# A transformer kernel: the memory cross-attention in three float32r products, with GpSimd making two of the low parts

## What is computed

```python
def memory_cross_attention(h, mem_n, w_mem_q, w_mem_kv, w_mem_o):
    q = jnp.einsum("bsd,de->bse", h, w_mem_q).reshape(B, S, MEM_HEADS, MEM_HEAD_DIM)
    kv = jnp.einsum("bmd,de->bme", mem_n, w_mem_kv)
    k = kv[..., :D_MODEL].reshape(B, M, MEM_HEADS, MEM_HEAD_DIM)
    v = kv[..., D_MODEL:].reshape(B, M, MEM_HEADS, MEM_HEAD_DIM)
    s = jnp.einsum("bshd,bmhd->bhsm", q, k).astype(jnp.float32) * (MEM_HEAD_DIM ** -0.5)
    p = jax.nn.softmax(s, axis=-1).astype(v.dtype)
    o = jnp.einsum("bhsm,bmhd->bshd", p, v).reshape(B, S, D_MODEL)
    return jnp.einsum("bse,ed->bsd", o, w_mem_o)
```

## Time and profile before

| | |
|---|---|
| median of 3 runs | 1484.01 us (1483.98 to 1484.23) |
| the profiled execution | 1484.37 us, its span 1482.6 us |
| PE busy | 1440.1 us, 97% of the span |
| DVE, ACT, POOL busy | 851.4, 552.9 and 990.2 us |
| first score matmul to first matmul of `mem_o` | 1045.72 to 1077.01 us |

### The profile page before, as it was taken

One profiled execution on the slowest core, in us unless ns is written; L12 is line 12 of the kernel. 1 busy time (PEld: TensorE's weight loads), 2 busy tenths in 40 slices (PEclk: granted clock), 3 DMA queues, 4 the chain that ended last, 5 costly groups with the idle time before them and its releaser, 6 DMA issues.

```text
span 1482.6 us, 18612 instructions
## 1 busy us (share of the span) xinstructions
PE 1440.1 (97%) x6987; PEld 1169.7 (79%) x6987; DVE 851.4 (57%) x1334; ACT 552.9 (37%) x1075; POOL 990.2 (67%) x400
## 2 busy tenths in 40 slices
PE   3999999999999999999999999999999999999997
PEld 3888877778898888888898844789789888888886
DVE  6998156554565555666744786441516555465655
ACT  3201133433454344444333376452424523333214
POOL 1857554355668899888568996365153989788653
PEclk9999999999999999999999999999999999999999
DMA  9875321223543332322443200133024323232131
GB/s 349 298 270 209 100 85 57 86 86 106 169 153 114 114 113 87 114 86 85 156 126 109 86 1 1 59 125 123 7 86 142 114 86 114 86 114 86 57 97 74
DMA packets 103385, 167.88 MB, mean 113 GB/s; under 512 B 3917, under 2 KB 61185, under 8 KB 102785
## 3 DMA queue, kind: packets, MB, share of 16 engines
q1 hardware_dynamic: 100176, 160.45, 31.7%
q10 hardware_dynamic: 3121, 6.26, 1.4%
HBM read 161.97 MB, written 4.72 MB: 112 GB/s over the span
## 4 chain that ended last, share of the span: by engine, by line
PE 84%; DVE 10%; ACT 3%; DMA 2%; issue 1%; POOL 1%; DVEq 0%; SPq 0%; ACTq 0%; POOLq 0%
PE bank L911 25%; PE bank L913 25%; PE bank L912 25%; DVE bank L2054 2%; DMA ada_w<-in_w_ada 1%; DVE smx L2507 1%; DVE x L2050 1%; PE bank L1372 1%; PE bank L1429 1%; PE bank L1448 1%; DVE bank L2050 1%; PE bank L1183 1%; DVE m L2050 1%; ACT junk L1541 1%; PE bank L1195 1%
## 5 line engine op out<-in xcount | busy, mean ns | idle before, releaser
L911 PE MATMUL bank<-ht_hi,w_hi 128*128 128x512 f32 (+1 forms) x1200 | 442.9, 369 | 0.5 <-DVE ht_lo L2050 0.3
L912 PE MATMUL bank<-ht_hi,w_lo 128*128 128x512 f32 (+1 forms) x1200 | 440.1, 367 | 0.0
L913 PE MATMUL bank<-ht_lo,w_hi 128*128 128x512 f32 (+1 forms) x1200 | 440.0, 367 | 0.0
L759 POOL TENSOR_TENSOR w_lo<-w_raw,w_hi 128x2048 fp32r<-128x2048 f32 x83 | 389.8, 4697 | 6.9
L757 POOL TENSOR_SCALAR w_hi<-w_raw 128x2048 fp32r<-128x2048 f32 x83 | 162.3, 1955 | 343.5 <-DMA w_raw<-in_w_in 111.2
L911 PEld LDWEIGHTS bank<-ht_hi,w_hi 128*128 128x128 f32 x1200 | 226.5, 189 | 41.6 <-issue 2.7
L913 PEld LDWEIGHTS bank<-ht_lo,w_hi 128*128 128x128 f32 x1200 | 226.6, 189 | 37.1
L912 PEld LDWEIGHTS bank<-ht_hi,w_lo 128*128 128x128 f32 x1200 | 226.6, 189 | 36.8 <-issue 0.5
L809 POOL TENSOR_TENSOR dn_lo<-dn_raw,dn_hi_all 128x1024 fp32r<-128x1024 f32 x77 | 184.6, 2418 | 56.7 <-ACT dn_hi_all L1738 56.6
L2054 DVE SCALAR_TENSOR_TENSOR uc<-bank,par,uc 128x511 f32<-128x511 f32 x88 | 66.0, 750 | 128.7 <-ACT uc L1992 125.6
L823 POOL TENSOR_TENSOR dn_raw<-dn_raw 128x1024 f32<-128x1024 f32 x44 | 105.8, 2404 | 12.8 <-PE bank L913 4.8
(11 more groups left out here) (305 smaller groups left out, 2415.7 us busy)
## 6 DMA issues: line engine op xcount, KB each, us to landing
w_raw<-in_w_in SPq DMA_DIRECT2D x27, 1024.0 KB, 5.0
ada_w<-in_w_ada SPq DMA_DIRECT2D x48, 512.0 KB, 7.3
w_raw<-in_w_up SPq DMA_DIRECT2D x22, 1024.0 KB, 5.0
w_raw<-in_w_mlp_in SPq DMA_DIRECT2D x16, 1024.0 KB, 5.5
dn_raw<-in_w_mlp_out SPq DMA_DIRECT2D x28, 512.0 KB, 4.8
w_raw<-in_w_out SPq DMA_DIRECT2D x8, 1024.0 KB, 5.0
w_raw<-in_w_mem_kv SPq DMA_DIRECT2D x8, 1024.0 KB, 5.2
dn_raw<-in_w_down SPq DMA_DIRECT2D x16, 512.0 KB, 4.7
```

Source lines behind the costliest of these rows:

```text
L759: g.tensor_tensor(w_lo[:, r], w_raw[:, r], w_hi[:, r].bitcast(F32), ALU.subtract).then_inc(slab_split, 1)
L911: inc_free(pe.matmul(o, ah, bh, start=start, stop=False))
L912: pe.matmul(o, al, bh, start=False, stop=False)
L913: return pe.matmul(o, ah, bl, start=False, stop=stop)
```

## The change

It turns both products of the memory attention into `mm3`, and adds what feeds that:
- ACT, ahead of the query tiles, rounds `mem_k` and `mem_v` (128x2048 each) into `mem_k_hi` and `mem_v_hi`, which lie in the place of `mt_lo` and `mt_hi`, whose last use is over by then.
- POOL subtracts to make `mem_k_lo` and `mem_v_lo` (in the place of `mem_k` and `mem_v`), between the third and the fourth slab of `mem_q`.
- The query tiles are rounded by ACT into `qm_hi`; DVE makes `qm_lo` and only then is the bank free. PE's first score waits for all eight, and for `kv_lo`.
- The transposed tiles are rounded by ACT into `ptm`; DVE makes `ptm_lo`, in its list at the step t, and frees the bank.

```diff
@@ POOL
-            split_all(n, S0["ffn"] + 2)
+            split_all(n, S0["mem_q"] + 3)
+            g.wait_ge(kv_hi, 1)
+            g.tensor_tensor(mem_k_lo[:], mem_k[:], mem_k_hi[:].bitcast(F32), ALU.subtract).then_inc(kv_lo, 1)
+            g.wait_ge(kv_hi, 2)
+            g.tensor_tensor(mem_v_lo[:], mem_v[:], mem_v_hi.bitcast(F32), ALU.subtract).then_inc(kv_lo, 1)
+            split_all(S0["mem_q"] + 3, S0["ffn"] + 2)
@@ PE, scoresm and valuesm
-                        ins = pe.matmul(t.ap[:, 0:NM], qm[:, 2 * h + c, qt * P:qt * P + P], mem_k[:, 2 * h + c, :],
-                                        start=c == 0, stop=c == 1)
+                        q = slice(qt * P, qt * P + P)
+                        ins = mm3(t.ap[:, 0:NM], qm_hi[:, 2 * h + c, q], qm_lo[:, 2 * h + c, q],
+                                  mem_k_hi[:, 2 * h + c, :], mem_k_lo[:, 2 * h + c, :], c == 0, c == 1)
...
-                        ins = pe.matmul(t.ap[:], mem_v[:, kc, h * MHD + c * P:h * MHD + c * P + P], ptm_of[h % 2][:, kc],
-                                        start=kc == 0, stop=kc == MT - 1)
+                        d = slice(h * MHD + c * P, h * MHD + c * P + P)
+                        ins = mm3(t.ap[:], mem_v_hi[:, kc, d], mem_v_lo[:, kc, d], ptm_of[h % 2][:, kc],
+                                  ptm_lo[h % 2][:, kc], kc == 0, kc == MT - 1)
...
-            pe.wait_ge(k_back, 16)
+            pe.wait_ge(kv_lo, 2)
@@ ACT
-                            st.done(act.copy(pt[h % 2][:, kc], t.ap[:]), tile=t)
+                            st.done(act.copy(pt[h % 2][:, kc], t.ap[:]), ptm_made)
...
+            act.wait_ge(k_back, 16)
+            st.after()
+            st.done(act.copy(mem_k_hi[:], mem_k[:]), kv_hi)
+            st.done(act.copy(mem_v_hi, mem_v[:]), kv_hi)
             for m in range(DC):
-                copy_out(T0["mem_q"] + m, qm[:, m])
+                t = Tile(T0["mem_q"] + m)
+                t.wait_full(act)
+                st.done(act.copy(qm_hi[:, m], t.ap[:]), qm_made)
@@ DVE
+                    elif what == "t":
+                        for kc in range(MT):
+                            t = Tile(tiles["t", h] + kc)
+                            v.wait_ge(ptm_made, MT * h + kc + 1)
+                            tt(ptm_lo[h % 2][:, kc], t.ap[:], ptm_of[h % 2][:, kc].bitcast(F32), ALU.subtract, tile=t)
...
+            for m in range(DC):
+                v.wait_ge(qm_made, m + 1)
+                t = Tile(T0["mem_q"] + m)
+                tt(qm_lo[:, m], t.ap[:], qm_hi[:, m].bitcast(F32), ALU.subtract, tile=t)
```

More of the change, by code:

```diff
@@ L401, in build @@
             p1_sum = sb("p1_sum", [P, 2, T], where=lend)
-        mem_k = sb("mem_k", [P, DC, NM])
-        mem_v = sb("mem_v", [P, MT, D])
+        with ExitStack() as lend:
+            mem_k = sb("mem_k", [P, DC, NM], where=lend)
+            mem_v = sb("mem_v", [P, MT, D], where=lend)
+        mem_k_lo = sb("mem_k_lo", [P, DC, NM], F32R)
+        mem_v_lo = sb("mem_v_lo", [P, MT, D], F32R)
         mt_hi = sb("mt_hi", [P, DC, NM], F32R)
@@ L430, in build @@
         ph = ExitStack()
-        qm = sb("qm", [P, DC, T], where=ph)
+        qm_hi = sb("qm_hi", [P, DC, T], F32R, where=ph)
         pm = sb("pm", [P, 2, NT, NM], where=ph)
-        ptm = sb("ptm", [P, MT, T], where=ph)
+        ptm = sb("ptm", [P, MT, T], F32R, where=ph)
         gain5 = sb("gain5", [P, D], where=ph)
-        ptm_odd = sb("ptm_odd", [P, MT, T], where=ph)
+        ptm_odd = sb("ptm_odd", [P, MT, T], F32R, where=ph)
         ptm_of = (ptm, ptm_odd)
+        qm_lo = sb("qm_lo", [P, DC, T], F32R, where=ph)
+        ptm_lo = [sb(f"ptm_lo{i}", [P, MT, T], F32R, where=ph) for i in range(2)]
+        mem_k_hi = mt_lo
+        mem_v_hi = mt_hi[:].rearrange("p (a b) n -> p a (b n)", a=MT)
         ph.close()
@@ L471, in build @@
         squared, mlp_slab_hi, mlp_hi, mlp_sums = (sem(n) for n in ("squared", "mlp_slab_hi", "mlp_hi", "mlp_sums"))
+        qm_made, ptm_made, kv_hi, kv_lo = sem("qm_made"), sem("ptm_made"), sem("kv_hi"), sem("kv_lo")
         memory_kept, mt_back, k_back = sem("memory_kept"), sem("mt_back"), sem("k_back")
```

## The result

The change makes the kernel slower. Its median is 1490.3 us (1489.31 to 1492.0, 6 runs) beside 1484.12 us for the kernel before (6 runs): ratio 1.0036, interval 1.0024 to 1.0049. A second set of 6 runs gave 1489.55 us and 1.0034 (1.0022 to 1.0047). The forecast was 1488.9 us, with a range of 1484.8 to 1491.7. The profiled execution took 1489.31 us (forecast 1489.3); its span is 1487.3 us, 4.7 more than before.

The account below looks back on a forecast made before the run. PE bounds the attention before (31.29 us), DVE after the change: 1.83 us from DVE's list plus 3.07 from POOL's blocking is +4.90 on 1484.37, 1489.3 us profiled. The median, 0.36 us less, is 1488.9 us; range 1484.8 to 1491.7.

Parts of the forecast that it names:

- PE's products: Attention scores and values on PE: float32r matmuls take 22.42 us, 5.38 us less than before, a gain if PE stayed bound.
- The query tiles: Before the first score: DVE's last `qm_lo` is on the path and moves the score from 1045.72 to 1046.44, cost 0.72 us.
- Keys and values: Beside the query projection: ACT's two roundings and POOL's two subtractions of `mem_k` and `mem_v` cost nothing.
- the cover: Query projection: POOL's split of `mem_q`'s fourth slab ends over 4 us before PE needs it.
- DVE as the bound: Attention: DVE's 28.38 us up to the last `ptm_lo` sets the end, making the stage 1.83 us longer.
- The meeting with POOL: Attention: the slab freed early makes POOL's subtraction block DVE's first scaling of head 1's `pm`, 3.07 us.
- The sign as it was written: Profile after, attention: one `pm` scaling of over 3 us in POOL's split of a `mem_o` slab, all others 353 ns.
- Sum: End of the attention stage moves by 1.83 + 3.07 = +4.90 us, PE's -5.38 not counting.
- PE's waits in the stage: Attention: PE idle about 10 us in all, waiting for DVE's `pm` and `ptm_lo`, where there was none.
- the third rival: Attention: the waits also cost PE its clock, at worst o3's 2.72 us doubled; 1489 to 1491.7 us, chance 0.15.
- DVE keeps up: Attention: PE's gain is real and PE's list decides, -4.66 us, 1479.4 us; chance 0.10.
- DVE binds, but POOL does not disturb it: Attention: slab load comes late or the scaling isn't blocked, +1.83 us, 1485.8 us; chance 0.20.

Follow-up runs that it names:

- neg_pool: Changed kernel with POOL doing the 16 `pm` scalings and queries multiplied by -1/16, so a minimum replaces maximum and multiplication; stage 26.89 us, ratio 0.9968.
- after: The changed kernel itself, first set of runs and its profile, against the kernel before; stage 35.27 us, median 1490.3 us, ratio 1.0036.
- kv_late: Changed kernel with five in-place copies of `mem_k` on POOL ahead of its two new subtractions; stage 35.74 us, 1495.96 us in one run.
- hold_slab: Changed kernel with the freeing of `mem_q`'s last slab held back until the output projection's first matmul; stage 32.38 us, ratio 1.0016.
- after_again: The changed kernel run once more, nothing edited; stage 35.61 us, median 1489.55 us, ratio 1.0034.
- quarters: Changed kernel with POOL's subtraction for the `mem_o` slab that meets the attention cut into four of 128x512; stage 36.03 us, 1490.17 us in one run.
- neg_hold: Changed kernel with the slab's freeing held back and queries multiplied by -1/16, so a minimum replaces maximum and multiplication; DVE scales `pm`; stage 30.87 us, ratio 1.0000.
- before_early: Kernel before with only the signal that frees `mem_q`'s last slab moved to the first score; stage 33.90 us, ratio 1.0019.
- pool_scales: Changed kernel with all 16 scalings of `pm` done by POOL, DVE making only the reciprocals; stage 29.36 us, ratio 0.9997.

## Why the prediction was right

The chain of causes that it forecast is the one that ran; by its steps:

- *PE's products.* 0.12 and 0.227 us apart, as taken; neg_pool's stage of 26.89 us, 4.40 less than before, shows at least that much of the 5.38 us as real once PE is the bound. In after none of it is left: DVE sets the end.
- *The query tiles, +0.72.* The first score came 0.61 us later, the projection's end 0.09 earlier: 0.70.
- *Keys and values, 0.* ACT's two casts took 1.90 and 1.91 us (bound 2.1), POOL waited 1.29 us for the next slab after its subtractions (1.3 forecast), and kv_late measured the cover.
- *DVE as the bound.* hold_slab is this step alone. From the prediction's terms, 1.00 + 28.38 + 0.3 + 2.72 = 32.40 us; measured 32.38.
- *The meeting with POOL, +3.07.* 2.90 us in after, 3.23 in the second trace, 2.89 between the stages of after and hold_slab. The prediction allowed that the copy catches head 0's last scaling too and "adds nothing"; that is what happened in after. It added nothing because DVE then reached head 1's first scaling later, and still got free at the same moment. The sign as it was written, one scaling of over 3 us, is not in the profile of after; it is in that of after_again.
- *Sum.* 1046.44 + 35.47 (1.00 + 28.38 + 3.07 + 0.3 + 2.72) = 1081.91 against 1081.60 in the trace. That the profiled execution came within 0.01 us of 1489.3 is luck: it was the fastest of six. The median, 1490.3, lies 1.4 us above the forecast, on the upper edge of the 1487.3 to 1490.3 that the forecast kept for itself.

Off were two side remarks. PE's waits in the stage were forecast at about 10 us and are 6.5; half clock fills 1.7 us of the difference (the transposes and values from 1059.78 to 1065.07 took 5.29 us, at full clock 0.87 + 12 x 0.227 = 3.59). And the third rival, that waits cost PE its clock, was right in its mechanism and wrong in its price here: the clock did fall, under DVE's cover. In quarters, neg_hold and kv_late it fell on the path: 0.5 us (7.99 us from the last head's transposes to `mem_o`, 7.47 in after), 1.0 (o2 ended at 1075.0, DVE's signal was due at 1074.0) and 2.6. The rivals "DVE keeps up" and "DVE binds, but POOL does not disturb it" are excluded by PE's waits, by the two long scalings, and by hold_slab and before_early, which take the meeting away and bring it about.

## What to carry to other kernels

A cheaper product on the engine that binds is worth only what the next engine has to spare: before halving PE's work in a stage, add up the other engines' lists back to back, as for 28.38 us here, and if one of them becomes the bound, shorten that list in the same step (neg_pool). Look at what rides on the instructions that are replaced: here a signal that frees a buffer moved 31 us forward, and the load and the split that it sets off cost 2.9 us of the stage, more than the rest of the change, and 2.6 us on the kernel before. A wait is dear twice if PE's clock falls behind it; a chain that hides the wait today need not hide the clock tomorrow.

## What the runs showed of the hardware

- DVE's scaling out of and into SBUF stands still while POOL runs a copy or a subtraction of SBUF tiles: it was 1.44 (before_early) to 1.70 us (quarters) longer behind a copy, 1.30 (before_early) to 3.39 us (kv_late) behind a subtraction of a whole slab. Beside the same POOL instructions DVE's reductions out of PSUM took 0.41 to 0.43 us as always, and `qm_lo`, a subtraction with one operand in PSUM, 0.69 us beside POOL's subtraction from 1041.00 to 1045.58 (after).
- POOL takes 484 ns for a 128x256 scaling in SBUF, DVE 353; and POOL's copy of 128x2048 is 1.9 us, its subtraction 4.6.
- The clock was at half (1.2 GHz) behind PE waits of 1.76 (neg_hold), 2.10 (after), 2.16 and 2.21 (quarters), 3.98 (after_again), 3.64 and 4.14 us (kv_late), and stayed full behind 2.41 (after), 2.43 (pool_scales), 2.47 (kv_late) and 2.81 us (hold_slab).
